# Stacked low-rank factors for the gate logits, and another order at launch, in a two-block transformer kernel

## What is computed

```python
h = rms_norm(x, ln_mix_pre[i])
proj = h @ w_in
q, k, v, g, glr = jnp.split(
    proj, [GLA_DK, 2 * GLA_DK, 2 * GLA_DK + GLA_DV, 2 * GLA_DK + 2 * GLA_DV], axis=-1)
log_a = jax.nn.log_sigmoid((glr @ w_gate_up + b_gate_up).astype(jnp.float32)) / GLA_GATE_NORMALIZER
```

## Time and profile before

| | |
|---|---|
| timed runs | 1978.97, 1981.17, 2941.43 us; median 1981.17 |
| the profiled execution | time 1978.7 us, span 1976.9 us, mean granted clock 0.999 |
| TensorE matmuls | 1964.7 us busy, 99% of the span |
| VectorE | 1186.3 us busy, 60% |
| ScalarE | 839.4 us busy, 42% |

### The profile page before, as it was taken

How to read it: one execution, slowest core, us unless ns; L and a number is a source line. 1 busy time by engine, 2 the same in 40 slices (tenths; PEclk the granted TensorE clock), 3 DMA queues, 4 the chain that set the end, 5 groups by cost and what they waited for, 6 DMA issues and landing times.

```text
span 1976.9 us, 25033 instructions
## 1 busy us (share of the span) xinstructions
PE 1964.7 (99%) x9778; PEld 1618.8 (82%) x9778; DVE 1186.3 (60%) x1795; ACT 839.4 (42%) x1363; POOL 12.6 (1%) x18
## 2 busy tenths in 40 slices
PE   9999999999999999999999999999999999999999
PEld 8777888888888788888888987777788888888887
DVE  4445754444466765444445686777897547774764
ACT  4534443323245744323323427777534334442431
POOL 0000000000000000000000000000000000000000
PEclk9999999999999999999999999999999999999999
DMA  5222232323233113232422332222232313232321
GB/s 197 71 86 79 86 96 75 118 96 121 72 113 133 53 57 109 91 106 71 142 86 86 107 107 80 82 86 86 86 96 96 128 44 112 99 98 75 117 96 64
DMA packets 51895, 188.03 MB, mean 95 GB/s; under 512 B 5762, under 2 KB 6018, under 8 KB 51139
## 3 DMA queue, kind: packets, MB, share of 16 engines
q1 hardware_dynamic: 51778, 186.43, 28.2%
HBM read 184.31 MB, written 2.10 MB: 94 GB/s over the span
## 4 chain that ended last, share of the span: by engine, by line
PE 96%; DVE 2%; ACT 1%; issue 0%; DMA 0%; SPq 0%; DVEq 0%; ACTq 0%
PE ps L396 19%; PE ps L397 19%; PE ps L398 19%; PE ps L425 10%; PE ps L426 10%; PE ps L427 10%; PE ps L447 1%; PE ps L861 1%; PE ps L894 1%; PE ps L875 1%; PE ps L839 1%; PE ps L780 1%; PE ps L766 1%; ACT PW L1290 0%; PE ps L751 0%
## 5 line engine op out<-in xcount | busy, mean ns | idle before, releaser
L396 PE MATMUL ps<-HH,WH 128*128 128x512 f32 (+1 forms) x1776 | 659.2, 371 | 1.0 <-DVE V L1777 0.6
L398 PE MATMUL ps<-HH,WL 128*128 128x512 f32 (+1 forms) x1776 | 650.6, 366 | 0.0
L397 PE MATMUL ps<-HL,WH 128*128 128x512 f32 (+1 forms) x1776 | 650.5, 366 | 0.0
L1028 ACT ACTIVATE WH<-WR 128x1024 fp32r<-128x1024 f32 x305 | 321.0, 1058 | 652.3 <-PE ps L398 374.1
L1631 DVE TENSOR_TENSOR WL<-WR,WH 128x1024 fp32r<-128x1024 f32 x304 | 370.1, 1224 | 192.9 <-ACT WH L1028 186.3
L396 PEld LDWEIGHTS ps<-HH,WH 128*128 128x128 f32 x1776 | 335.0, 189 | 62.4 <-issue 8.8
L397 PEld LDWEIGHTS ps<-HL,WH 128*128 128x128 f32 x1776 | 335.1, 189 | 54.5 <-issue 1.9
L398 PEld LDWEIGHTS ps<-HH,WL 128*128 128x128 f32 x1776 | 334.9, 189 | 54.7
L425 PE MATMUL ps<-WH,HIDH 128*128 128x512 f32 x620 | 241.6, 390 | 0.0
L426 PE MATMUL ps<-WH,HIDL 128*128 128x512 f32 x620 | 241.2, 389 | 0.0
L427 PE MATMUL ps<-WL,HIDH 128*128 128x512 f32 x620 | 241.2, 389 | 0.0
(11 more groups left out here) (243 smaller groups left out, 2007.5 us busy)
## 6 DMA issues: line engine op xcount, KB each, us to landing
WR<-in_up SPq DMA_DIRECT2D x108, 512.0 KB, 3.6
WR<-in_down SPq DMA_DIRECT2D x86, 512.0 KB, 3.5
WR<-in_in SPq DMA_DIRECT2D x56, 512.0 KB, 3.5
WR<-in_swa_in SPq DMA_DIRECT2D x10, 512.0 KB, 4.6
WR<-in_gla_in SPq DMA_DIRECT2D x9, 512.0 KB, 4.5
WR<-in_gla_v SPq DMA_DIRECT2D x8, 512.0 KB, 3.4
WR<-in_gla_g SPq DMA_DIRECT2D x8, 512.0 KB, 4.4
WR<-in_gla_out SPq DMA_DIRECT2D x8, 512.0 KB, 3.5
```

Of the source, the lines that this page charges most:

```text
L396: e.matmul(ps, wh, hi[:, c, cols], start=c == 0, stop=False)
L397: e.matmul(ps, wh, lo[:, c, cols], start=False, stop=False)
L398: y = e.matmul(ps, wl, hi[:, c, cols], start=False, stop=c == x.n - 1)
L1028: e.activation(x.wh[:, 0:n], m.WR[:, u % RAW, 0:n], AF.Copy).then_inc(*k.mark("whi", u))
```

## The change

Gate logits. The tile of `glr` now holds its 16 columns four times (at 0, 32, 64 and 96). `v_cut` replaces the last copy by the low part of the weights. So four stacked groups of rows come out of `low_rank`: the high part's product three times, and the low part's once. VectorE's `evac(4)` writes all 128 rows into GLR, rounded to fp32r, with ones in rows 16 and 80, then writes what the rounding left of rows 32 to 63 into these. WGU has four copies of the factor, the bias in rows 16 and 80 of the first and third. ScalarE writes it rounded as WGH, and VectorE replaces rows 64 to 95 of WGH by what the rounding left (mark `wgl`). The four matmuls of z then have 128 rows of fp32r on both sides. Added up over the rows they give the high factor by the high, low by high, high by low, and the weights' low part by high. TensorE waits for `wgl`.

Launch. The low part WL of the first weight tile comes ahead of both groups of the second token tile's HL on VectorE, where it was between them. `busy(2)` before the first turn becomes `busy(4)`, and `busy(2)` before the second becomes `busy(3)`.

```diff
-    m.GLR = over("GLR", [64, T], gains)
-    m.WGU = over("WGU", [64, T], gains + 2 * KB)
+    m.GLR = over("GLR", [128, T], gains, F32R)
+    m.WGU = over("WGU", [128, T], gains + 2 * KB)
+    m.WGH = over("WGH", [128, T], dg + 2 * KB, F32R)
...
-    busy(2)
+    busy(4)
     t_turn(e, k, "mix0", 0)
-    busy(2)
+    busy(3)
     t_turn(e, k, "mix0", 1)
     busy(4)
...
-            e.wait_ge(*k.on("wgu"))
+            e.wait_ge(*k.on("wgl"))
...
-                e.matmul(ps[4 + t][:, :], m.GLR[:, tile(t)], m.WGU[:, :], start=True,
+                e.matmul(ps[4 + t][:, :], m.GLR[:, tile(t)], m.WGH[:, :], start=True,
...
         a_cut(e, k, u + j + 3)
+        if j == 2:
+            e.wait_ge(*k.on("wgu"))
+            e.activation(m.WGH[:, :], m.WGU[:, :], AF.Copy).then_inc(*k.mark("wgh"))
...
-            e.tensor_tensor(wh[:, :, 32:48], raw[:, :, 0:16], wh[:, :, 0:16].bitcast(F32), A.subtract).then_inc(
+            e.tensor_tensor(wh[:, :, 96:112], raw[:, :, 96:112], wh[:, :, 96:112].bitcast(F32), A.subtract).then_inc(
...
         elif j == 4:
+            rows = slice(32, 64)
             e.wait_ge(*k.on("const"))
-            e.tensor_scalar(m.GLR[:, :], p[0:64, :], cst(m, "ident")[0:64, 16:17], None, A.add).then_inc(*k.mark("ev", u + j))
+            e.tensor_scalar(m.GLR[:, :], p, cst(m, "ident")[:, 16:17], cst(m, "ident")[:, 80:81], A.add, A.add).then_inc(
+                *k.mark("glr"))
+            e.wait_ge(*k.on("glr"))
+            e.tensor_tensor(m.GLR[rows, :], p[rows, :], m.GLR[rows, :].bitcast(F32), A.subtract).then_inc(
+                *k.mark("ev", u + j))
+            rows = slice(64, 96)
+            e.wait_ge(*k.on("wgh"))
+            e.tensor_tensor(m.WGH[rows, :], m.WGU[rows, :], m.WGH[rows, :].bitcast(F32), A.subtract).then_inc(
+                *k.mark("wgl"))
...
     v_split(e, k, "mix0", 0)
-    v_split(e, k, "mix0", 1, (0,))
     v_cut(e, k, u)
-    v_split(e, k, "mix0", 1, (1,))
+    v_split(e, k, "mix0", 1)
...
-    L["gla_in"] = tiles(np.concatenate([wi[:, 3072:3088], np.zeros((D, 112), wi.dtype), wi[:, 512:1024], wi[:, 0:512]],
-                                       1))[:, 0]
+    low = np.concatenate([wi[:, 3072:3088], np.zeros((D, 16), wi.dtype)], 1)
+    L["gla_in"] = tiles(np.concatenate([low] * 4 + [wi[:, 512:1024], wi[:, 0:512]], 1))[:, 0]
...
-    g = np.zeros((2, 32, T), np.float32)
+    g = np.zeros((4, 32, T), np.float32)
     g[:, 0:16] = a["gla_w_gate_up"][0]
-    g[0, 16] = a["gla_b_gate_up"][0]
-    L["wgu"] = g.reshape(64, T)
+    g[0::2, 16] = a["gla_b_gate_up"][0]
+    L["wgu"] = g.reshape(128, T)
```

More of the change, by code:

```diff
@@ L1651, in v_normed, with v_split @@
         *k.mark("y", tag, t))
-def v_split(e, k, tag, t, groups=(0, 1)):
+def v_split(e, k, tag, t):
     m, b = k.m, turn_bank(tag, t)
-    for g in groups:
+    for g in range(2):
         hh = m.HH[:, 4 * g:4 * g + 4, tile(t)]
```

## The result

| | before | after |
|---|---|---|
| median of 20 runs | 1980.39 us | 1977.97 us |
| lowest, highest | 1978.71, 5111.1 | 1974.21, 1978.71 |
| the profiled execution: time, span | 1978.7, 1976.9 | 1978.08, 1976.3 |

The ratio of the two kernels is 0.9985 (95% interval 0.9978 to 0.9991): 0.15% less, clear of noise and far inside 2%. It leaves out two executions of the kernel before that took far longer than the rest (2941.43 and 5111.1 us). The medians of the table differ by 2.4 us (0.12%), and the two spans by 0.6 only. Both are right, and why they differ is the main finding of this study.

What follows compares the result with a forecast made beforehand. The prediction took TensorE to bound the kernel, with matmuls on 99% of the span. Logits -2.9 and launch -0.05 took the profile's 1978.7 to 1975.75; on the base of 1978.97 it forecast 1976.0 us, range 1973.5 to 1981.

Steps and rivals of the forecast that it cites:

- if the spans differ by less than 2 us: Sign that the forecast is wrong, comparing the profiled executions before and after; more than 4.5 us was the other limit.
- The logits: -2.9: Gate logits on TensorE: four z matmuls at 0.226 us each instead of 0.91, plus 0.1 at the change of kind.
- Nothing for the three steps on VectorE, ScalarE's copy and the transfer: Added work around the gate logits costs TensorE nothing; VectorE done about 47.7, z could start at 48.36, 0.7 us spare.
- No wait behind it eats the gain: TensorE's five waits from 12 to 250 us, 2.6 us in all, start earlier with it and eat no gain.
- case B: Launch: clock falls at 7.78 again, added ones use up the earlier WL, first product starts at 14.35; 0.05 us gained.
- Case A: Launch: the clock does not fall, so the first product starts at 13.5; 0.9 us gained.
- R1: Rival at launch: the clock holds because the ones fill 0.40 us of idleness; 1975.2 us, chance 0.27.
- the base: Starting time for the sum: 1978.97 us, the middle of three usable readings of the kernel before.
- R3: Rival at launch: clock stays low past 11.10, first product 3.1 us late; 1980.8 us, chance 0.07.
- R2: Rival at the gate logits: z waits for wgl, losing 0.4 to 1.5 us; 1976.4 to 1977.5 us, chance 0.1.
- R4: Rival at the gate logits: z's matmuls run no faster, some operand keeping four steps; 1978.9 us, chance 0.02.

Runs made afterwards that it cites:

- stack_alone: Stacked gate logits alone put into the kernel before, launch order and ones unchanged; median 1977.48 us against 1980.54, ratio 0.9983.
- launch_alone: WL order and the three added matmuls of ones alone put into the kernel before; median 1980.89 us against 1980.54, ratio 1.0002.
- gain_rows128: Changed kernel with 2 and 2 ones, gains brought into 128 partitions and spread by 128-row matmuls; 1976.84 us, ratio 0.9983 to the kernel before.
- zero_rows: Changed kernel with 2 and 2 ones, gains spread by 128-row matmuls, 127 rows zero, constants transferred first; 1976.01 us, ratio 0.9979 to the kernel before.
- fewer_ones: Changed kernel without ones before the first turn and between the two turns; 1976.44 us, ratio 0.9981 to the kernel before.
- no_ones: Changed kernel without any matmul of ones, the first three and last four left out too; 1977.92 us, ratio 0.9989 to the kernel before.
- zero_rows_fewer: Changed kernel with zero_rows' 128-row gains matmuls, but no ones around the turns; 1975.06 us, ratio 0.9975 to the kernel before.

## Why the prediction was right, and where it was not

The forecast was 0.15% less, and the ratio measured is 0.9985. The time forecast was 1976.0 against 1977.97, inside the range of 1973.5 to 1981. That the two percentages are the same is in part luck: the logits gave what was forecast, the launch took back some of it, and the medians alone differ by 0.12%. And by a sign that the prediction itself had named, it is wrong: "if the spans differ by less than 2 us". They differ by 0.6, and the first product starts at 16.72, at neither of the two times it gave (14.3 to 14.4, or 13.5). The experiments show that this comes from which execution was profiled, and not from the logits.

- **The logits: -2.9.** Right. The same stretch is 2.87 shorter in the trace, and stack_alone gives 3.0 to 3.1 in either group. The step of 0.226 us from the neighbours held (0.91 for four), as did the 0.1 at each change of kind. Like with like, the whole sum held: for the profiled kind of execution it said 1975.75, and the three runs of after with a recorded fall took 1975.5 to 1975.9.
- **Nothing for the three steps on VectorE, ScalarE's copy and the transfer.** Right: they were priced to end 0.7 us ahead of z and ended 0.71 ahead. A subtraction over 32 partitions costs what one over 128 costs (0.68), as I had assumed with 0.69. WGU landed 9.7 us after its issue (10.3 before) although it had twice the bytes.
- **No wait behind it eats the gain.** Right, the list above. (The 2.6 us that the prediction wanted compared between 60 and 250 us are those from 12 us on; between 60 and 250 it is 2.2 before and 2.1 after.)
- **The launch, case B: -0.05.** Right as a mechanism: in launch_alone, caught with a recorded fall, the first product starts right behind the last ones, as forecast, at 14.45 where 14.35 was worked out, and its one run of that kind is 0.25 over before's median of that kind. That it fits to 0.1 is partly luck. The clock fell at about 7.5 and not at 7.78, and the turns began at 8.84 and 12.04 where 8.28 and 11.74 were worked out; the clock also rose earlier, at about 10.9, and the product followed the last ones more closely than assumed, which gave most of it back. Case A seems to exist as well: three of 20 runs took 1974.2 to 1974.6, where it had said 1975.2. None of them was profiled; by the sum under the table their first product started at about 13, an estimate. R1's reason, that the ones fill the idle 0.40 us, is not enough: in launch_alone they fill it and the clock falls.
- **The step that failed is the base.** "Of the three usable readings 1978.7, 1978.97 and 1981.17 the middle one is 1978.97" took two draws of the rarer group for the usual time. The usual one is 1980.4; with it the same sum would have said 1977.5. And the cases A and B both took for granted that the clock is high from 4.4 us on, since it was in the one trace. In the larger group (75 of 104 runs of before, as read from the late profiles of its neighbours) it rises much later, the gains take 3.8 us, and the matmuls of ones stand in the way of a turn that is ready. That case was on no list. In it the launch edits cost about 0.4 us (1981.03 against 1980.62), which the intervals don't tell from nothing, but which is most of the difference between -2.9 and the -2.4 measured. R3, a low clock that stays on, had the price about right (0.81 for each matmul of ones, against 0.89 in the late executions) and the place wrong: ahead of the rise, not behind a second fall.
- **R2 and R4** fell: no wait names WGH or GLR, and the four matmuls of z run as their neighbours do.

The hint was there. I had quoted the Trainium skill, "TensorE: Matmul & The Clock Gate", Part 1, that the watch over activity is not reset when a kernel starts, and had let it choose only between A and B. The runs agree with that rule in that executions of one kernel differ in it (the groups of 1974.2, 1975.4 and 1977.7 us and up among 20 runs), and show that what varies is above all when the clock first rises.

## What to carry to other kernels

A small plain float32 product whose factors can be split may be stacked along empty rows of the array: its four terms then cost one reduced-precision pass, here 0.23 us per matmul of 512 columns instead of 0.91, and the added splitting is free where VectorE waits. Matmuls put in as a filler are queued work: at the low clock each of these cost 0.8 to 0.9 us, so they belong only where nothing that is ready stands behind them. And before a profile is taken as the base, see in which group of its kernel's run times it lies; two executions of one kernel that differ at launch by 2 us can hide, or fake, a change of 3.

## What the runs showed of the hardware

- The granted clock reads 1.00 ahead of the first fall that the trace records, also while matmuls take twice their time (3.77 for four records of 512 columns against 1.98).
- A matmul with one row runs as long as one with 128 (3.77 and 3.78 us for four records at the low level, 1.98 for either at the high one), but in what follows they differ. After four records with one row at the low level, the ones behind them were still at the low level in every profile of that group (2.07 to 2.08 us for four records of ones, or 3.78 for eight); after four with 128 rows they were at the high level or rose within them (1.24 in gain_rows128, 1.55 in zero_rows). Rows that hold zeros did so in their profile as rows with data did, though their slowest runs were slower (1977.5 against 1977.0); 32 rows did not do (2.08 behind them). These are seven late profiles with one row (ones stand behind the gains in five of them, in fewer_ones and no_ones turns, also at half pace), two with 128 and one with 32, together with the run times, and not a rule.
- The fall of the clock needs no idle time just ahead of it: in launch_alone TensorE ran without a gap from 4.45 us, and the clock fell at about 7.5. Nor need an idle gap bring it about: in zero_rows_fewer it held through 1.46 and 0.94 us.
- Between kernels without ones, with few and with many, no choice took the spread away: the one with the lowest median still ran from 1974.2 to 1977.5.
